# One core, one fused two-block forward pass: the second block's first adaptation on VectorE, and two attention units sent earlier

## The reference, cut to what matters

```python
for l in range(DEPTH):
    h = rms_norm(x, ln1_gain[l])
    proj = h @ w_in[l]
    # o_nsa: compressed, selected and windowed attention; o_mla: attention over latents; o_ret: retention
    mixed = jnp.concatenate([o_nsa, o_mla, o_ret], axis=-1)
    x = x + mixed @ w_out[l]
    h = rms_norm(x, ln2_gain[l])
    x = x + jnp.square(jax.nn.relu(h @ w_up[l])) @ w_down[l]
```

```python
def adaln(cond, w, b):
    m = jax.nn.silu(cond) @ w + b      # cond: two vectors of 1024, w: 1024 x 3072
    return jnp.split(m, 3, axis=-1)
```

## Time and profile before

| what | us |
|---|---|
| median of three runs | 1077.58 (1077.52 to 1077.97) |
| span of the profiled execution, first to last instruction | 1076.1 |
| TensorE busy in it | 1051.7 (98%) |
| VectorE busy | 751.0 (70%) |
| ScalarE busy | 549.1 (51%) |
| mixers of layer 0, of layer 1 (start of the first transposes) | 73.42, 406.62 |
| first attention scores of layer 0, of layer 1 | 105.63, 438.83 |
| feed-forward of layer 0 (first product to last) | 161.36 to 340.02 |

### The profile page before, as it was taken

The page is one execution under the profiler, slowest core; times in us unless marked ns, Lnnn a source line. Parts: engine busy times, 40 slices in busy tenths (PEclk is TensorE's granted clock), DMA queues, the critical chain, the costliest instruction groups (busy, mean ns, idle before and its releaser), DMA issues. The chain is left out here.

```text
span 1076.1 us, 17324 instructions
## 1 busy us (share of the span) xinstructions
PE 1051.7 (98%) x6788; PEld 900.5 (84%) x6788; DVE 751.0 (70%) x1442; ACT 549.1 (51%) x993; POOL 63.4 (6%) x80
## 2 busy tenths in 40 slices
PE   8999999999999999999999999999999999999996
PEld 7877889899988886888998899888886687989865
DVE  5766757655556576777788888789898945824765
ACT  5543845544445454764444544452657833623563
POOL 1000000000000000001000000020051301000000
PEclk9999999999999999999999999999999999999998
DMA  9758056565564657325856566593326233943200
GB/s 344 263 197 344 3 157 195 162 201 191 192 196 163 196 196 266 120 84 185 185 196 196 160 199 197 189 305 133 110 93 260 78 118 107 257 140 118 60 21 40
DMA packets 55477, 183.33 MB, mean 170 GB/s; under 512 B 21092, under 2 KB 33764, under 8 KB 35940
## 3 DMA queue, kind: packets, MB, share of 16 engines
q1 hardware_dynamic: 55396, 182.22, 51.8%
HBM read 179.31 MB, written 2.90 MB: 169 GB/s over the span
## 5 line engine op out<-in xcount | busy, mean ns | idle before, releaser
L257 DVE TENSOR_TENSOR w_lo<-ring,w_hi 128x1024 fp32r<-128x1024 f32 x259 | 316.2, 1223 | 179.8 <-ACT w_hi L242 176.2
L242 ACT CAST w_hi<-ring 128x1024 fp32r<-128x1024 f32 x259 | 270.9, 1054 | 318.0 <-PE banks L313 317.5
L313 PE MATMUL banks<-f_hi,w_hi 128*128 128x256 f32 x512 | 144.0, 281 | 0.0
L313 PE MATMUL banks<-f_hi,w_lo 128*128 128x256 f32 x512 | 143.8, 281 | 0.0
L313 PE MATMUL banks<-f_lo,w_hi 128*128 128x256 f32 x512 | 143.8, 281 | 0.0
L313 PE MATMUL banks<-w_hi,u_hi 128*128 128x512 f32 x256 | 100.1, 391 | 0.0
L313 PE MATMUL banks<-w_hi,u_lo 128*128 128x512 f32 x256 | 99.9, 390 | 0.0
L313 PE MATMUL banks<-w_lo,u_hi 128*128 128x512 f32 x256 | 99.9, 390 | 0.0
L313 PEld LDWEIGHTS banks<-f_hi,w_hi 128*128 128x128 f32 x512 | 96.4, 188 | 0.7 <-DVE f_lo L444 0.2
L313 PEld LDWEIGHTS banks<-f_lo,w_hi 128*128 128x128 f32 x512 | 96.5, 188 | 0.5
L313 PEld LDWEIGHTS banks<-f_hi,w_lo 128*128 128x128 f32 x512 | 96.5, 188 | 0.0
(11 more groups left out here) (421 smaller groups left out, 2167.9 us busy)
## 6 DMA issues: line engine op xcount, KB each, us to landing
ring<-in_w_up SPq DMA_DIRECT2D x32, 1024.0 KB, 5.2
ring<-in_w_down SPq DMA_DIRECT2D x32, 1024.0 KB, 5.1
ring<-in_w_in SPq DMA_DIRECT2D x23, 1024.0 KB, 5.2
ring<-in_ab_ada SPq DMA_DIRECT2D x12, 1024.0 KB, 5.9
ring<-in_cd_ada SPq DMA_DIRECT2D x12, 1024.0 KB, 5.2
ring<-in_cd_in SPq DMA_DIRECT2D x12, 1024.0 KB, 5.6
ring<-in_w_out SPq DMA_DIRECT2D x8, 1024.0 KB, 7.5
ring<-in_ab_in SPq DMA_DIRECT2D x16, 512.0 KB, 4.8
```

Source lines behind the costliest of these rows:

```text
L242: nc.scalar.copy(w_hi[:, n % PARTS, :], part_source(key, q)).then_inc(hi_ready, 1)
L257: nc.vector.tensor_tensor(w_lo[:, n % PARTS, :], part_source(key, q), w_hi[:, n % PARTS, :].bitcast(F32), ALU.subtract).then_inc(part_read ...
L313: mm = nc.tensor.matmul(dst, a, b, start=first_one and i == 0, stop=last_one and i == 2, skip_group_check=shares_bank)
```

## The change

Two things change. The first adaptation leaves the mixers: its twelve halves are now loaded between the halves of the first feed-forward (`ADA_BEHIND`), and VectorE accumulates weight times condition there, two operations of 128x512 behind most parts (`adapt_on_vector`). TensorE sums the partitions at that stage's end (`sum_partitions`, three times), ScalarE copies the sums out, SP writes them to DRAM, and the next stage reads them back as columns (`columns_of_rows`). The square behind the ReLU moves from VectorE to ScalarE in both feed-forwards, and so does one sum of squares in the first. In the mixers of both layers the three slabs and their copies are gone, and the attention is cut in two: the scores of units 0 and 1 are sent before the compressed values, VectorE takes their maxima there, and ScalarE takes their exponentials behind its third group of copies. For that the retention's result moves to banks 4 and 5, which makes each value product wait for all five faded heads, and the groups of transposes use two banks in place of three.

```diff
+ADA_SLABS = 3 * D // BANK
+ADA_BEHIND = [3 + (9 * m + 2) // 4 for m in range(2 * ADA_SLABS)]
...
+        def adapt_on_vector(dve, sums_of, done):
+            n = 0
+            for m, i in enumerate(ada_at):
+                for kk in range(KC // 2):
+                    k = m % 2 * (KC // 2) + kk
+                    w = ring[:, i % SLOTS, kk * BANK:(kk + 1) * BANK]
+                    if kk == 0:
+                        half_here(dve, i)
+                    for v in range(2):
+                        to, factor = sums_of[:, m // 2, v, :], cond[:, k, v:v + 1]
...
+                            dve.wait_ge(done, n - 1)
+                            last = nc.vector.scalar_tensor_tensor(out=to, in0=w, scalar=factor, in1=to, op0=ALU.mult,
+                                                                  op1=ALU.add)
...
+        def sum_partitions(pe, sums_of, r, bank):
+            for j in range(COL_GROUPS):
+                rows = slice(j * GROUP_COLS, (j + 1) * GROUP_COLS)
+                mm = nc.tensor.matmul(banks[rows, bank, :], minus_half[:, 0:1].broadcast_to([P, GROUP_COLS]),
+                                      sums_of[:, 2 * r + j // 2, j % 2, :], start=True, stop=True)
+            return mm
+
+        def columns_of_rows(sp):
+            sp.wait_ge(rows_out, 16 * COL_GROUPS)
+            for v in range(2):
+                sp.dma_start(ada[:, 0, :, v], row_sums[v].rearrange("r s n -> (r s n)").rearrange("(c p) -> p c", p=P),
+                             allow_slow_non_contiguous=True).then_inc(columns_here, 16)
...
                 def values_of(h):
-                    pe.wait_ge(faded_ready, max(h + 1, TT))
+                    pe.wait_ge(faded_ready, RET_H)
...
                 here["values"](pe)
-                adapt_products(pe, ada_key, 0, ADA)
...
                 turn_heads(0)
-                pe.wait_ge(mix_kept, 1)
-                turn_heads(1)
+                begin_attention()
                 pe.wait_ge(cmp_probs_copied, 1)
...
             def banks_here(pe):
-                pe.wait_ge(mla_copied, 4)
+                pe.wait_ge(mla_copied, len(groups))
                 pe.wait_ge(retained_ready, 1)
...
                     last.then_inc(mla_copied, 1)
-                attend_scalar(act)
+                    if g == 2:
+                        begin_attention()
+                attend()
...
+                    if not beside:
+                        sp.wait_ge(rows_kept, 2)
+                        for j in range(COL_GROUPS):
+                            sp.dma_start(row_sums[j % 2:j % 2 + 1, :, j // 2, :],
+                                         summed_rows[j * GROUP_COLS:j * GROUP_COLS + 1, :, :]).then_inc(rows_out, 16)
...
                     if not beside:
-                        keep_busy(0, 4)
+                        pe.wait_ge(adapted, 96)
+                        sum_partitions(pe, ada_sums, 2, 2).then_inc(rows_summed, 1)
                         return
...
+                        nc.scalar.activation(square[:], relu[:], ACT.Square).then_inc(square_ready, 1)
...
-                        nc.vector.tensor_tensor(square[:], relu[:], relu[:], ALU.mult).then_inc(square_ready, 1)
```

More of the change, by code:

```diff
@@ L101, in slab_plan @@
 def slab_plan():
-    halves, first, first_part, n_parts = [], {}, {}, 0
+    halves, first, first_part, half_at, ada_at, n_parts = [], {}, {}, {}, [], 0
     uses = [((name, layer), name, layer * n, n) for layer in range(DEPTH) for name, n in LAYER_SLABS]
@@ L209, in load_first_part, with load_behind @@
             sp.dma_start(ring[:, 0, cols], dram[name][at, :, cols]).then_inc(first_parts_here[q], 16)
-        def load_behind(sp, key, n_slabs, halves=2):
-            for i in range(first[key], first[key] + halves * n_slabs):
+        def load_behind(sp, key, n_slabs, between=0):
+            for i in range(first[key], first[key] + 2 * n_slabs + between):
                 load_half(sp, i + SLOTS)
@@ L1396, in values, with begin, rest, vector_programs @@
                     mm.then_inc(values_ready, 1)
[L1398 to L1406, removed]
-                keep_busy(0, 4)
-            def vector_program(dve):
+                def begin():
+                    scores(0)
+                def rest():
+                    banks_here(pe)
+                    for i in range(1, n_units + VALUES):
+                        if i % 2 == 1 and i + 1 < n_units:
+                            scores(i + 1)
+                        if TURN <= i < n_units + TURN:
+                            turn(i - TURN)
+                        if i >= VALUES:
+                            values(i - VALUES)
+                    keep_busy(0, 4)
+                return begin, rest
+            def vector_programs(dve):
                 noted = [0]
@@ L1464, in vector_program, with steps, rest, scalar_programs @@
                 more = iter(()) if aside is None else aside(aside_vector, aside_done)
[L1465 to L1470, removed]
+                def steps(first_one, end):
+                    for i in range(first_one, end):
+                        step_both(i, i - WEIGH)
+                        advance(more, 1)
+                def rest():
+                    steps(2, n_units + WEIGH)
+                    advance(more)
+                return lambda: steps(0, 2), rest
+            def scalar_programs(act):
                 def exponential(i):
@@ L2201, in _ @@
                 def _(sp):
-                    for i in range(first["ada_turn", layer], first["ada_mix", layer]):
+                    for i in range(first["cmp_k", layer], first["w_out", layer]):
                         load_half(sp, i + SLOTS)
@@ L2687, in down @@
                             mm.then_inc(part_used, 1)
+                            if not beside and i == 2 * FFN_GROUPS - 1 and q == 0:
+                                pe.wait_ge(relu_ready, FFN_GROUPS)
+                                pe.wait_ge(adapted, 64)
+                                for r in range(2):
+                                    sum_partitions(pe, ada_sums, r, r).then_inc(rows_summed, 1)
                     norm["tensor"](pe)
```

152 lines of the change are left out of this document (84 added, 68 removed).

## The result

| | before | after |
|---|---|---|
| median, us (four runs each, side by side) | 1077.78 (1077.52 to 1078.77) | 1090.67 (1088.14 to 1091.46) |
| ratio | | 1.0112 (1.0100 to 1.0124) |
| span of the profiled execution | 1076.1 | 1086.4 |
| TensorE busy | 1051.7 | 1049.8 |
| mean granted TensorE clock | 0.997 | 0.987 |

The change made the kernel 1.1% slower. TensorE has 2 us less to do by its busy time, and the clock row says why that is no gain: busy time counts a product for as long as it takes, and some took twice as long. The profiled execution (1088.14 us) is the fastest of the four; all four have a mean granted clock of 0.984 to 0.987.

A forecast was written before the change was run, and what follows sets the result against it. TensorE's own work was taken as the bound in the first feed-forward. Mixers -5.4, sums +1.9 and stage's end +2.4 gave -1.1; 1076.1 - 1.1 + 1.5 = 1076.5 us, range 1073.0 to 1080.2.

The forecast's parts named there:

- the clock rival: TensorE's clock falls to 0.50 in the new waits (retention, first feed-forward's end): 1079.3 to 1086 us; chance 0.10.
- the sum: Whole kernel: mixers -5.4, sums inside the feed-forward +1.9, that stage's end +2.4, together -1.1 us, giving 1076.5 us.
- The rival's price for all three waits: Stage's end and both retentions: one part of 2.79 and twice 3.4 us of value products at half clock, +9.6, 1086 us.
- The mixers' sum: Mixers of each layer: slabs and turns removed and the early pair gain 2.7 us a layer, 5.4 in two.
- The stage's end: End of the first feed-forward: ScalarE's copy 0.55 and four write issues ahead of the barrier, +2.4 us with semaphores.
- Neither price of the prediction: SP's write issues at the first feed-forward's end: 0.43 us each was taken, 1.22 the alternative, giving +5.5.
- The two sums: First feed-forward: two partition sums inside a part on TensorE, 0.95 us each, hidden by nothing, +1.9 us.
- VectorE kept pace: First feed-forward: new operations 0.67 us each, VectorE hidden at 11.6 of 12.56; rival that it becomes the bound, chance 0.08.
- The single-element reads: Next projection: two reads of 3072 single elements, taken as covered; rival that they hold up the ring, 1089 us, chance 0.05.
- The range: Whole kernel: 1073.0 to 1080.2 us, leaving out some 0.2 of the chance.
- the clock's far end: All three new waits followed by work at half clock: +9.6, 1086 us, the extreme of a case given 0.10.

The follow-up runs named there:

- the run with the early sums: Changed kernel with all three partition sums inside the last slab but three parts and four fillers at the first feed-forward's end: 1087.10 us, ratio 1.0089.
- the filled run: Changed kernel with nine small unused products in front of the retention's value products in each layer: 1082.44 us, ratio 1.0042.
- four fillers: Changed kernel with four small unused products, not nine, in front of the retention's value products: 1087.34 us, ratio 1.0090.
- the one with the late pair: Changed kernel with scores, maxima and exponentials of units 0 and 1 behind everything else again, retention's result still in banks 4 and 5: 1085.99 us, ratio 1.0073.

## Why the prediction was wrong

**The step that failed** is the clock rival's "Against: the wait in the retention is the shorter, and no row shows a fall between two pieces of work." With it the sum put the clock behind the new waits at nothing. The wait was known, 2.1 us, right to 0.05. What it does was taken from one row behind the last product, and from nothing between pieces of work in a kernel whose own waits between pieces of work were 1.2 us at most. With the wait alone put into the kernel before, both layers fell. That no trace shows a fall is weak evidence where no trace shows such a wait; the rival deserved more than 0.10. Its sign was wrong as well: it asked for 0.50 at the first work behind the wait, and here that work began at 1.00 and the fall came 2.4 us later.

**What the falls cost.** With the wait filled, layer 0's mixers last 58.54 us; with it, 62.69, and layer 1's 62.75. The next projection lasts 1.13 us longer than where the clock held. That is 4.15 + 4.21 + 1.13 = 9.5 of the 10.3 us, if layer 1 at full clock takes what layer 0 takes. The rival's price for all three waits, 2.79 + 2 x 3.4 = 9.6, is as large, but by luck: the part at the stage's end was too high, and the falls in the mixers reach beyond the value products, over all that comes next. The median execution is 2.5 us slower than the profiled one, at a lower mean clock, so in it the falls probably cost more.

**What is left**, 0.8 us, stands against the -1.1 of the sum: 1.55 too little for the stage's end, 0.7 too little for the feed-forward, 0.3 too much for each layer's mixers, and 0.9 us gained that weren't in it.

**The mixers' sum was right at full clock** within 0.3: -2.4 in layer 0 with the wait filled, -2.7 forecast. That the second pair leaves at 104.95 to the hundredth has some luck in it, since the value products start 0.1 earlier than written and the keys' copies take 1.48 us, not 1.34.

**The stage's end was mis-sized.** +2.4 was taken, it is 5.30 - 1.35 = +3.95: 0.70 an issue, and 0.8 from the last issue to the restart, which the 0.30 between two rows did not show. Neither price of the prediction is that of such an issue. 0.43 is a read into SBUF; 1.22 is the mean of two issues that took 0.43 and 1.97 and so the length of neither. That the source of the writes lies in SBUF doesn't explain their length either: the writes of the result out of SBUF, at the end of the kernel before, take 0.34 each. Why these take 0.70 isn't shown.

```profile
1072.56 0.34 SPq L2867 DMA_DIRECT2D out<-mixed  x1
```

**The two sums** take 334.11 to 335.96, 1.85; 1.9 was forecast. From the stage's first product to its last the distance grew by 2.55 (163.16 to 344.37 against 161.36 to 340.02): 0.42 of the 0.70 between them is a wait for a split, below, and some 0.3 I have not placed.

**VectorE kept pace.** In the middle of the stage it is busy 89 us of 100, TensorE 100, and the transfer engines' share is 0.80, as forecast. Near the stage's start TensorE waited 0.42 us once for one of VectorE's splits (190 to 200: busy 9.58 of 10). VectorE had waited 1.41 us there for ScalarE's high part, which stood behind the square and the sum of squares that moved to ScalarE. The sum put that at nothing. Groups of the first feed-forward, VectorE's timeline, and two stretches, after:

```profile
L378 DVE SCALAR_TENSOR_TENSOR ada_sums<-ring,cond_pad,ada_sums 128x512 f32<-128x512 f32 x84 | 59.3, 747 | 3.1 <-DVE w_lo L267 1.3
```

```profile
193.46 1.22 DVE L267 TENSOR_TENSOR w_lo<-ring,w_hi 128x1024 fp32r<-128x1024 f32 x1 [1.41 <-ACT w_hi L252]
...
306.95 1.41 DVE L378 SCALAR_TENSOR_TENSOR ada_sums<-ring,cond_pad,ada_sums 128x512 f32<-128x512 f32 x2
308.28 1.22 DVE L267 TENSOR_TENSOR w_lo<-ring,w_hi 128x1024 fp32r<-128x1024 f32 x1
```

```profile
190.00:200.00 10.00, 9.58 (x53) 7.90 (x52) 8.30 (x10) 6.45 (x9) 0.89 (x2) 1.00 0.65 215
200.00:300.00 100.00, 100.00 (x663) 92.01 (x662) 89.48 (x106) 50.30 (x49) 0.00 (x0) 1.00 0.80 276
```

308.28 - 306.95 is 1.33 for two, 0.67 each, the value taken; a single record lists 0.75 with its overlap. **The single-element reads** held up nothing: SP issued both in 3.0 us (350.11), and where the clock held, in the run with the early sums, the next projection lasts 65.25 us as before.

**The range**, 1073.0 to 1080.2, left out the clock's far end knowingly, for a chance of 0.10. That was the main error. With the retention's falls gone and two shorter ones left, the filled run still lies 2.2 us above the range; those two and the stage's end are enough to account for it.

## What to carry to other kernels

Before a filler is taken off TensorE's row, work out what it stands in front of: if another engine sets the start of what follows, the time doesn't come back, and the wait that appears can cost more than itself, because the clock falls behind it and slows all that comes next. Here 2.11 us of wait in each layer's retention went with some 4 us a layer lost to the clock. The length of the wait alone did not say whether this happens (2.41 us at the stage's end did not do it), so price a new wait with and without a fall, and read the granted clock behind it in a trace. Take the wait away by what it waits for (here two banks), and fill what is left with products nobody needs.

## What the runs showed that I had not expected

**The fall need not lie in the wait.** In the retention work resumes at 94.06 and the stretch from 94 to 96 is still at 1.00. Of the eight such waits of 2.1 us in the profiled executions, seven were followed by a fall 0.4 to 2.4 us behind the restart; in one (layer 0 of the kernel before with the wait) the clock fell 0.4 us ahead of the restart. In the wait of 4.24 us at the stage's end it fell 0.7 us ahead of the restart in the changed kernel and 1.5 ahead with four fillers, but 0.2 behind it in the run with nine.

**The wait alone doesn't decide.** Waits of 2.1 us in the retention were followed by a fall in every profiled execution that had them (the changed kernel, the one with early sums, the one with the late pair, the kernel before with the wait: both layers each). Waits of 2.41 and 2.42 us at the stage's end were not, in two kernels. Waits of 0.4 to 1.3 us were followed by one in some layers and not in others, with the same rows ahead, and in the kernel before by none. How long the low level lasted ranged from 3.4 to 10.2 us. What decides stays open.
